# A hybrid attention and mixture-of-experts block on one core: the router reads unnormed rows, and its steps are spread over the stage

## The reference

```python
x = x + jnp.concatenate([o_a, o_b], axis=-1) @ w_out[l]
h2 = _rmsnorm(x, norm2_g[l]).reshape(B * S, D)
x = x + _moe(h2, router_w[l], router_b[l], w_up[l], b_up[l], w_down[l], b_down[l])
return _rmsnorm(x, final_norm_g)

def _moe(h, router_w, router_b, w_up, b_up, w_down, b_down):
    logits = h @ router_w + router_b            # 512 x 32
    top_vals, top_idx = lax.top_k(logits, 4)
    gates = softmax(top_vals)
    ...
    def expert_block(xb, e):
        u = xb @ w_up[e] + b_up[e]
        return _clamped_swiglu(u) @ w_down[e] + b_down[e]
```

## Time and profile before

| | us |
|---|---|
| median of 3 runs (lowest, highest) | 1464.61 (1462.31, 1465.46) |
| the profiled execution | 1461.71 |
| its span in the trace | 1459.9 |
| TensorE busy | 1364.3 (93%) |
| VectorE busy | 1179.7 (81%) |
| ScalarE busy | 1052.1 (72%) |
| chain that ended last: TensorE 72%, DMA 8%, ScalarE 8%, issue 6%, VectorE 5% | |

### The profile page before, as it was taken

One profiled execution on the slowest core, in us unless ns is written; L12 is line 12 of the kernel. 1 busy time (PEld: TensorE's weight loads), 2 busy tenths in 40 slices (PEclk: granted clock), 3 DMA queues, 4 the chain that ended last, 5 costly groups with the idle time before them and its releaser, 6 DMA issues.

```text
span 1459.9 us, 19587 instructions
## 1 busy us (share of the span) xinstructions
PE 1364.3 (93%) x6347; PEld 1068.3 (73%) x6348; DVE 1179.7 (81%) x1029; ACT 1052.1 (72%) x885; POOL 293.4 (20%) x137
## 2 busy tenths in 40 slices
PE   6999989896899999999999999999999999999992
PEld 5778866565687777777777777777777777777771
DVE  5347645448789999898999989898989999898983
ACT  6344333223588989797988989797888989797962
POOL 0000000001014142433212122121215141134410
PEclk9999999985899999999999999999999999999996
DMA  7313144342699999999999999999999999999964
GB/s 231 87 58 100 46 164 183 123 163 96 237 361 389 405 396 417 398 414 402 407 408 391 416 399 415 397 413 399 404 409 404 406 394 416 398 415 397 403 224 145
DMA packets 99320, 464.55 MB, mean 318 GB/s; under 512 B 9211, under 2 KB 37907, under 8 KB 50067
## 3 DMA queue, kind: packets, MB, share of 16 engines
q1 hardware_dynamic: 91906, 438.11, 74.7%
q0 software_dynamic: 7376, 25.96, 7.1%
HBM read 443.85 MB, written 20.19 MB: 318 GB/s over the span
## 4 chain that ended last, share of the span: by engine, by line
PE 72%; ACT 8%; DMA 8%; issue 6%; DVE 5%; ACTq 0%; SPq 0%; DVEq 0%; POOLq 0%
PE psum L1652 46%; PE psum L1442 7%; DMA w_raw<-w_up 5%; ACT w_high L735 4%; PE psum L1439 3%; PE psum L1668 2%; DVE w_low L1282 2%; ACT up_fold L749 2%; PE psum L1635 2%; PE psum L1645 2%; PE psum L1572 2%; PE psum L1528 1%; PE psum L1683 1%; PE psum L1552 1%; DMA w_buf<-w_out 1%
## 5 line engine op out<-in xcount | busy, mean ns | idle before, releaser
L1282 DVE TENSOR_TENSOR w_low<-w_raw,w_high 128x2048 fp32r<-128x2048 f32 x384 | 862.4, 2288 | 82.0 <-ACT w_high L735 81.7
L735 ACT ACTIVATE w_high<-w_raw 128x2048 fp32r<-128x2048 f32 x384 | 719.0, 1912 | 150.9 <-PE psum L1652 127.7
L1652 PE MATMUL psum<-w_high,x_high 128*128 128x512 f32 x1024 | 278.7, 394 | 0.0
L1652 PE MATMUL psum<-w_low,x_high 128*128 128x512 f32 x1024 | 274.6, 390 | 0.0
L538 POOL COPY gather_rows<-row_t 128x1 int32 (+1 forms) x33 | 50.4, 1527 | 868.2 <-PE psum L1635 528.1
L1652 PEld LDWEIGHTS psum<-w_high,x_high 128*128 128x128 f32 x1024 | 191.0, 189 | 44.7 <-issue 5.4
L1652 PEld LDWEIGHTS psum<-w_low,x_high 128*128 128x128 f32 x1024 | 192.7, 188 | 40.8
L1652 PE MATMUL psum<-w_high,a_high 128*128 128x512 f32 x512 | 162.6, 399 | 0.0
L1652 PE MATMUL psum<-w_low,a_high 128*128 128x512 f32 x512 | 158.7, 391 | 0.0
L1652 PE MATMUL psum<-w_high,x_low 128*128 128x512 f32 x544 | 151.4, 400 | 0.0
L549 POOL DMA_INDIRECT residual_rows<-y_rows,scatter_rows x32 | 92.6, 2895 | 231.6 <-ACT y_rows L774 225.0
(11 more groups left out here) (274 smaller groups left out, 1419.9 us busy)
## 6 DMA issues: line engine op xcount, KB each, us to landing
w_raw<-w_up SPq DMA_DIRECT2D x256, 1024.0 KB, 13.1
w_raw<-w_down SPq DMA_DIRECT2D x128, 1024.0 KB, 13.4
w_in_raw<-w_in SPq DMA_DIRECT2D x28, 512.0 KB, 3.7
w_buf<-w_out SPq DMA_DIRECT2D x2, 2048.0 KB, 10.9
x_rows<-x SPq DMA_DIRECT2D x4, 512.0 KB, 4.6
x_rows<-x SPq DMA_DIRECT2D x1, 2048.0 KB, 18.5
residual_rows<-x_rows SPq DMA_DIRECT2D x4, 512.0 KB, 2.6
normed_rows<-h_rows SPq DMA_DIRECT2D x4, 512.0 KB, 2.6
```

Source lines behind the costliest of these rows:

```text
L735: act.activation(wh[:, q.slot(m, SPL), :], raw[q.slot(m, RAW)][:, :], ACT.Copy).then_inc(wh_ready, 1)
L1282: dve.tensor_tensor(wl[q.slot(m, RAW)][:, :], raw[q.slot(m, RAW)][:, :], wh[:, q.slot(m, SPL), :].bitcast(F32), ALU.subtract).then_inc(wl_ ...
L1652: ins = pe.matmul(o[:, j, :], x_part, w_part[:, j * 512:(j + 1) * 512], start=(first and n == 0), stop=(last and n == len(passes) - 1))
```

## The change

- **Router on unnormed rows.** The weights of the router are multiplied once by the norm's g (the g comes in with the other vectors, transposed to columns `g2c`). TensorE transposes X and not H2 (`rows_turned`), and VectorE multiplies the logits by the row's inverse root and adds the bias (`rb_rows`, on 128 partitions) in the instruction that reads them. The product with the bias row goes. The square is taken in two halves.
- **Selection and places by tile.** `choose(t)` does the selection of a tile when its logits are there; TensorE's `places(t)` adds its part to the count.
- **First expert by constants.** Expert 0's selection matrix is made straight from the places, and its rows come from a product with a constant (`tok_one`), before the gates are known. Expert 1's own selection goes; it comes with all others from `turns`.
- **Order in the first expert.** Gates, `turn_values`, `turn_sels`, `turn_rows` and `order_experts` stand between the splits of the first expert; `x_low(1)` and `swiglu(0)` stand before the fourth split of the second expert, and not before the sixth.
- **Biases.** Loaded ahead of the first weights into another place, and split by 512 columns in each of the heads 2 to 7. Weights 4 and 5 are loaded behind the attention, and three weights behind the first gather.
- **ScalarE** rounds the first weight before the squares and the second behind the third tile's root; before the second it waits until the normed rows of tiles 0 and 1 are written to memory, before the third for those of tiles 2 and 3.

The diff, cut to its core:

```diff
-            for n in range(6):
+            for n in range(2):
+                sp.dma_start(bias_raw[n * NE:(n + 1) * NE, 0:NF], b_up).then_inc(S("bias_in"), 16)
+                sp.dma_start(bias_raw[n * NE:(n + 1) * NE, NF:NF + D], b_down).then_inc(S("bias_in"), 16)
+            for n in range(4):
                 load(FIRST, n, n, 0)
             sp.wait_ge(S("attn_read"), AH)
             sp.dma_start(G2[:, :], norm2_g.to_broadcast([P, D])).then_inc(S("g2_in"), 16)
-            sp.dma_start(bias_raw[0:NE, 0:NF], b_up).then_inc(S("bias_in"), 16)
-            sp.dma_start(bias_raw[0:NE, NF:NF + D], b_down).then_inc(S("bias_in"), 16)
-            sp.dma_start(bias_raw[NE:2 * NE, 0:NF], b_up).then_inc(S("bias_in"), 16)
-            sp.dma_start(bias_raw[NE:2 * NE, NF:NF + D], b_down).then_inc(S("bias_in"), 16)
-            load(FIRST, 6, 6, 0)
-            load(FIRST, 7, 7, 0)
+            for n in range(4, UPC):
+                load(FIRST, n, n, 0)
...
+            sp.wait_ge(gathered, 16)
...
+            full(act, "xa", 2 * TT - 1)
+            cast(FIRST, 0, 0)
+            for i in range(TT):
+                for n in range(2):
+                    freed(act, "x2", i, n)
+                    c = slice(n * 512, (n + 1) * 512)
+                    act.activation(H2[:, i, c], X[:, i, c], ACT.Square, accum_out=ss2[:, i, n:n + 1]).then_inc(S("ss2"), 1)
+                    if i and n == 0:
+                        router_half(i - 1, 1)
+                act.wait_ge(S("mean_eps"), 3 + i)
+                root(act, r2[:, i:i + 1], mean2[:, i:i + 1])
+                if i == TT - 2:
+                    for t in range(2):
+                        act.wait_ge(S(f"normed_out{t}"), 16)
+                    cast(FIRST, 1, 1)
+            router_half(TT - 1, 1)
+            act.activation(warm[:, 3:4], warm[:, 0:1], ACT.Exp).then_inc(S("tables"), 1)
+            act.wait_ge(S("lg_shifted"), 1)
+            act.activation(LG[:, 1, :], LG[:, 1, :], ACT.Exp).then_inc(S("lg_exp"), 1)
+            for t in range(2, TT):
+                act.wait_ge(S(f"normed_out{t}"), 16)
+            cast(FIRST, 2, 2)
+            cast(FIRST, 3, 3)
             x_high(X0)
-            act.wait_ge(S("turn_sels"), 1)
+            cast(FIRST, 4, 4)
...
+                if 2 <= h:
+                    if h == 2:
+                        dve.wait_ge(S("bias_in"), 64)
+                    c = slice((h - 2) * 512, (h - 1) * 512)
+                    link(dve.tensor_copy(bias_hl[:, c], bias_raw[:, c]))
+                    link(dve.tensor_tensor(bias_hl[NE:2 * NE, c], bias_raw[NE:2 * NE, c], bias_hl[NE:2 * NE, c].bitcast(F32), ALU.subtract))
+                if h == 1:
+                    dve.wait_ge(S("rw_in"), 16)
+                    dve.tensor_tensor(rw_sb[:, :, :], rw_sb[:, :, :], spread(g2c, NE), ALU.mult).then_inc(S("router_scaled"), 1)
+                    link(dve.memset(pos_t[:, :, :], -1.0))
+                    link(dve.memset(vals_t[:, :, :, :], 0.0))
...
+            def normed(i):
+                dve.scalar_tensor_tensor(H2[:, i, :], X[:, i, :], r2[:, i:i + 1], G2[:, :], ALU.mult, ALU.mult).then_inc(S("h2_rows"), 1)
...
+            def choose(t):
+                tile = slice(t * NE, (t + 1) * NE)
+                logit, fourth, allowed, same = LG[:, 0, tile], top8[:, t, TOPK - 1:TOPK], rt[:, 0, t:t + 1], rtmp[:, 8:8 + TOPK]
+                full(dve, "lg", t)
+                dve.scalar_tensor_tensor(logit, bank("lg", t)[:, 0:NE], r2[:, t:t + 1], rb_rows[:, :], ALU.mult, ALU.add
+                                         ).then_inc(free_sem("lg", t), 1)
+                freed(dve, "lg", t)
+                link(dve.max(top8[:, t, :], logit))
+                link(dve.tensor_scalar(LG[:, 3, tile], logit, fourth, None, ALU.is_equal))
+                link(dve.tensor_scalar(same, top8[:, t, 0:TOPK], fourth, None, ALU.is_equal))
+                link(dve.tensor_tensor_scan(LG[:, 4, tile], ones[:, 0:NE], LG[:, 3, tile], 0.0, ALU.mult, ALU.add))
+                link(dve.tensor_reduce(allowed, same, AX.X, ALU.add))
+                link(dve.scalar_tensor_tensor(LG[:, 4, tile], LG[:, 4, tile], allowed, LG[:, 3, tile], ALU.is_le, ALU.mult))
+                dve.scalar_tensor_tensor(LG[:, 2, tile], logit, fourth, LG[:, 4, tile], ALU.is_gt, ALU.add).then_inc(S("selected"), 1)
...
+                freed(dve, "xa", 2 * i)
+                add_share("x2", i, 0)
+                if i:
+                    router_half(i - 1)
+                freed(dve, "xa", 2 * i + 1)
+                add_share("x2", i, 1)
+                if i == TT - 1:
+                    router_half(i)
+                row_mean(i)
+                if i:
+                    choose(i - 1)
+                row_root(i)
+                if i < TT - 1:
+                    normed(i)
+                if i == 1:
+                    split(FIRST, 0)
+            choose(TT - 1)
+            normed(TT - 1)
...
+            def first_rows():
+                dve.wait_ge(t_full, SEL0 + 1)
+                link(dve.tensor_scalar(rtmp[:, 16:17], Tflat[:, 1:2], cst("minus_p"), cst("dump_row")[:, 0:1], ALU.mult, ALU.add))
+                dve.tensor_tensor(row_t[:, 0:1], Tflat[:, 0:1], rtmp[:, 16:17], ALU.add).then_inc(slot_ready, 1)
+                dve.tensor_copy(gate_t[:, 0:1], Tflat[:, 1:2]).then_inc(t_free, 1)
...
-            make_sel(0)
+            first_rows()
             bias_row(BSU, of_expert(0), bsu_ready)
-            slot_rows(SEL0, 0)
-            make_sel(1)
-            order_experts()
-            split(FIRST, 0)
-            ordered()
-            slot_rows(SEL1, 1)
             split(FIRST, 1)
+            slot_values()
             split(FIRST, 2)
             x_low(0)
             split(FIRST, 3)
+            dve.wait_ge(S("acc_out"), 16 * TT)
+            gates()
             turn_values()
+            split(FIRST, 4)
             turn_sels()
-            for n in range(4, UPC):
-                split(FIRST, n)
-                if n == 6:
-                    turn_rows()
+            split(FIRST, 5)
+            turn_rows()
+            split(FIRST, 6)
+            order_experts()
+            split(FIRST, 7)
             for n in range(NC):
-                if n == 5:
+                if n == 3:
                     x_low(1)
                     swiglu(0)
+                if n == 4:
+                    ordered()
...
+                for k in range(4):
+                    c = (4 * n + k) * P
+                    ins = pe.transpose(o[:, k, :], X[:, i, c:c + P], ident)
+                ins.then_inc(full_sem("h2T", i, n), 1)
+            def logits(i):
+                o = begin("lg", i)[:, 0:NE]
                 for n in range(2):
+                    freed(pe, "h2T", i, n)
+                for k in range(DK):
+                    ins = pe.matmul(o, H2T[:, i % 2, k, :], rw_sb[:, k, :], start=(k == 0), stop=(k == DK - 1))
+                ins.then_inc(full_sem("lg", i), 1)
+            def places(t):
+                o = begin("pos") if t == 0 else bank("pos")
+                counts_of = o[:, 0:(TT + 1) * NE].rearrange("p (t e) -> p t e", e=NE)
+                sel = LG[:, 2, t * NE:(t + 1) * NE]
+                pe.wait_ge(S("selected"), t + 1)
+                pe.matmul(counts_of[:, t, :], cst("before"), sel, start=(t == 0), stop=False, skip_group_check=True)
+                ins = pe.matmul(counts_of[:, t + 1:, :], ones, sel.unsqueeze(1).broadcast_to([P, TT - t, NE]), start=False,
                                 stop=(t == TT - 1), skip_group_check=True)
+                if t == TT - 1:
+                    ins.then_inc(full_sem("pos"), 1)
+            for i in range(TT):
+                attn_share(i, 0)
+                if i:
+                    rows_turned(i - 1, 0)
+                    rows_turned(i - 1, 1)
+                if i == TT - 1:
+                    for t in range(TT - 2):
+                        places(t)
+                attn_share(i, 1)
+                if i == TT - 1:
+                    rows_turned(i, 0)
+                if i:
+                    logits(i - 1)
+            rows_turned(TT - 1, 1)
+            logits(TT - 1)
+            places(TT - 2)
+            places(TT - 1)
...
-            select(0, SEL0, 0)
-            order()
-            select(1, SEL1, 1)
+            pe.wait_ge(sel_ready, TT)
+            for i in range(TT):
+                ins = pe.matmul(Tflat[:, 0:2], SEL[:, i, :], cst("tok_one")[:, 2 * i:2 * i + 2], start=(i == 0), stop=(i == TT - 1))
+            ins.then_inc(t_full, 1)
```

246 lines of the change are left out of this document (100 added, 146 removed).

## The result

| | kernel before | changed kernel |
|---|---|---|
| median, 20 runs each | 1462.87 us | 1468.30 us |
| ratio, 95% interval | | 1.0032 (1.0022 to 1.0043) |
| span of the profiled execution | 1459.9 us | 1465.5 us |

The forecast was 1454.3 with a range to 1460.0, so both its sign and its range were wrong. The places at which the prediction made its sum show where it went. The last column is the version with all repairs that the experiments end with. A profiled execution may start the products of its attention stage up to 4 us later than another (216.1 to 220.3 us in the profiles here), so a difference of a few microseconds between two places of two profiles means little; lengths between two places of one profile are steadier.

A forecast was written before the change was run, and what follows sets the result against it. TensorE was taken to pace the expert stage, a full DMA queue close behind, so the gain was its earlier start: +1.9 - 10.9 - 3.0 + 1.7 = -10.3, from 1464.61 to 1454.3 us, range 1447.5 to 1460.0.

The forecast's parts named there:

- Step 1: Attention stage: bias splits delay the first share by 3.2 us, three of six exposed at 1.05 each; bounds 0 to 6.3.
- rival (a): TensorE's clock stays up from the last logits on: 1451.3 us to the row numbers, 1446 through expert 1; chance 0.10.
- Step 2: First share to end of the last share: gapless TensorE list, last share ends at 318.8, 1.9 us later than before.
- Step 3: Last share's end to expert 0's row numbers: 24.8 us becomes 13.9, a gain of 10.9.
- the stated sign: Before the row numbers: last logits taking 1.8 us and not 3.5 would show this stretch's forecast wrong.
- Step 4: Row numbers to expert 0's opening: 13.1 us becomes 10.1, with 5.7 for the gather; gain 3.0.
- Step 5: Expert 0's opening to expert 1's: 35.4 us becomes 37.1, VectorE setting the end behind `turns`; loss 1.7.
- the named sign again: At expert 1's opening: waiting for ScalarE and not for the low part would show this stretch's forecast wrong.
- The sum: From the front to expert 1's opening: +1.9 - 10.9 - 3.0 + 1.7 = -10.3 us.
- Behind it every step is as before: After expert 1's opening nothing changes in length; pairs of experts stay at 65.9 us.
- Rival (b): Expert stage gives the gain back if DMA sets its pace: half a microsecond per pair, 6.5 us, 1463; chance 0.05.
- Rival (c): Front: normed-row writes stuck behind loads delay ScalarE's second rounding and the gather, up to 21 us, 1472; chance 0.03.

The follow-up runs named there:

- the version with all repairs: Changed kernel with bias splits in covered places, expert ordering ahead of the first split, old addresses: 1448.32 and 1449.31 us, ratio 0.9902 to the kernel before.

## Why the prediction was wrong, step by step

**Step 1, the biases: 9.6 us where 3.2 was forecast; the main miss.** That three of the six are exposed, and at which places, was right. The waits grew by 1.29, 1.30 and 1.17, 3.8 in all, so 1.05 for each was close. The term that was missing is the clock: 1.70 + 1.70 + 2.08 = 5.5 us behind the three waits in this execution, and 0.95 more in the sixteen products that follow; that its attention stage began 0.6 us earlier takes as much off. This pair of profiles shows more than the usual: over all profiles the exposed splits cost 7.7 us, some 4 of them the clock. The prediction had the row that should have warned it, since it says in rival (a) that idle gaps of 1.26 to 1.48 us did not lower the clock. It then made exactly these gaps 1.1 us longer and priced only the wait. That row was itself one execution: in five of the seven profiles of the kernel before at other addresses the clock fell near the third of these waits, and the sixteen products took 8.5 to 8.8 us for 7.09. Covering the splits gave 7 us back.

**Step 2, the shares: right.** 325.0 - 289.4 = 35.6 against 35.8.

**Step 3, to the row numbers: right, 12.4 against 13.9.** The last logits took 1.96 and not 3.5, which was the stated sign that this term is wrong. That much of rival (a) came true in this execution; the clock fell only behind them, as the 0.56 of the window from 330 us shows. But it is a matter of the execution: of the twelve profiles with the changed front, eight have the last logits at 3.2 to 3.6 us and 13.6 to 14.0 to the row numbers, the second profile of the changed kernel among them, and four have 1.94 and 12.4. So the forecast's figure is the more frequent one.

**Step 4, to expert 0: 14.1 us where 10.1 was forecast.** The 1.3 + 4.4 for copy, issue and landing came from the earlier trace rows and from a first copy that ran beside short VectorE steps. The change put a split of 2.28 us right behind the row numbers and another soon after, and the copy (2.33) and the gather's issue (2.85 for 1.16, so that the rows land after 6.23) grew; the transfer behind the issue did not. The named sign, a gather that lands later than 4.4, showed it. Moving the split away gave 10.2. The Trainium skill ("Advanced Engine Details and Errata", section GPSIMD Details) says that the Pool engine shares a read and a write interface with VectorE and conflicts with its instructions that have two SBUF inputs; the split reads `w_raw` and `w_high`, both in SBUF, and the rows agree. The prediction did not weigh this, though the change moves just such an instruction beside GpSimd's.

**Step 5, to expert 1: 38.8 us where 37.1 was forecast.** Of the 1.7 us over, 1.2 come before `turns`: its products start 18.2 us behind the opening of expert 0 and not 17.0, since the first products of the expert ran longer at the lower level (the second and third group of four 1.91 and 1.78 us, where the kernel before had 1.36 and 1.08). The other 0.5 come behind it. Sixteen instructions and a split behind `turns` cost what was said, but VectorE's `x_low` did not set the end. TensorE stood 2.75 us for that split, the twelve products behind it took 4.61 us (2.86 in the kernel with the ordering moved, where no such wait comes), and so the transposes of expert 1's rows ended only at 387.25; ScalarE's `x_high`, `lin` and `sig` behind them set the opening, the named sign again. A wait and the clock behind it were left out here as in step 1. The second gather was hidden, as forecast: issued at 376.76, it landed at 382.7, 3.5 us ahead of the transposes.

**The sum.** The misses are 6.4 - 0.2 - 1.5 + 4.0 + 1.7 = +10.4, which cancels the forecast gain of 10.3 to the last tenth. That this left nothing is chance; each of the terms has its own cause.

**"Behind it every step is as before": wrong by 0.3%.** The address of every large buffer moved. By the runs, the same kernel at the old addresses is level (0.9997), and the old kernel at the new ones loses 0.23%. That the addresses do it is shown; by what mechanism is open. No step of the prediction asked what the longer constants and `small` do to the addresses. Rival (b) gave the stage's loss the size of the first pair of profiles, 0.4 us for each pair of experts (0.2 in the mean of all profiles), but the wrong cause: the order of work at its entry cost nothing. Its 1463 is 1463.9 by its own terms.

**Rival (c), writes stuck behind loads, did not occur.** ScalarE's second rounding began at 315.9 us, right behind the third tile's root and without a wait for the writes, and GpSimd's copy, which waits for all rows to be in memory, began 0.2 us behind the row numbers.

## What to carry to other kernels

When a diff changes the size of any buffer, give the changed kernel the old addresses and compare again before judging it; the loss here was 0.3%, with every large buffer 96 bytes higher. An added wait on the engine that TensorE waits for is priced twice, by its length (3.8 us here) and by the clock that may fall behind it (some 4 us here, and not the same in every execution), so put such work where TensorE has a list of its own. And what stands on VectorE beside a short GpSimd copy or an indirect transfer on the path should be short steps (0.22 us for the copy), not a long one with two SBUF inputs (2.33).

## What the runs showed of the hardware that was not expected

- The whole region 96 bytes higher costs 0.23% (1.0010 to 1.0036) with no instruction changed; -32, +32 and +64 bytes cost nothing that can be measured. In the mean of the profiles 2.4 us of it lie between the second and the last up fold. The cause is open.
- Moving `w_high`, or the slots and `w_high`, against the buffers of rows and activations made TensorE's own products 2% slower, 235.0 to 236.1 ns for 230.4, and took away nearly all of its idle time.
- Equal waits of 1.93 us let the clock fall once and hold once. Behind a wait of 2.77 us it was down in all six profiles of the exposed splits; behind one of 2.43 the first group was slow in one execution of the changed kernel (4.50) and quick (2.42) in the five others, a second execution of the same kernel among them, of which four had the clock down in the products that followed (8.78 for 7.09). Near a wait of 1.26 it fell in nine of thirteen profiles too. So one profile does not tell what a wait costs in clock.
- A GpSimd copy of one number per partition takes 0.22 us beside short VectorE steps and 2.33 beside a split; the indirect issue takes 1.16 or 2.85. From the end of the issue the first gather lands 3.2 to 3.4 us later either way.
